# Feed-forward with standing weights: gated values come out transposed from the third block on

## The reference

```python
def swiglu(h, w1, w3, w2):
    return (jax.nn.silu(h @ w1) * (h @ w3)) @ w2
...
    h = rms_norm(x, norm_ffn[i]) * (1.0 + sc2) + sh2
    x = x + g2 * swiglu(h, ffn_w1[i], ffn_w3[i], ffn_w2[i])
```

## Time and profile before

| | |
|---|---|
| runs | 863.06 us median (862.61, 863.06, 865.84) |
| profiled execution | 863.67 us, its span 861.9 us |
| TensorE matmuls | 835.1 us busy, 97% of the span, 4254 instructions |
| weight loads | 697.2 us, 81% |
| VectorE | 611.7 us, 71% |
| ScalarE | 432.4 us, 50% |
| GpSimd | 123.7 us, 14% |
| DMA | 188.98 MB, mean 219 GB/s |
| chain that ended last | TensorE 81%, line 516 alone 66% |

### The profile page before, as it was taken

One profiled execution on the slowest core, in us unless ns is written; L12 is line 12 of the kernel. 1 busy time (PEld: TensorE's weight loads), 2 busy tenths in 40 slices (PEclk: granted clock), 3 DMA queues, 4 the chain that ended last, 5 costly groups with the idle time before them and its releaser, 6 DMA issues.

```text
span 861.9 us, 10974 instructions
## 1 busy us (share of the span) xinstructions
PE 835.1 (97%) x4254; PEld 697.2 (81%) x4254; DVE 611.7 (71%) x749; ACT 432.4 (50%) x549; POOL 123.7 (14%) x154
## 2 busy tenths in 40 slices
PE   4999999999999999999999999999999999999998
PEld 2778888878878987888888887888888788887886
DVE  4897798787888776577566685787867756644544
ACT  5365464454535666443344366778575635434431
POOL 3000101111110100011010000467810000000000
PEclk9899999999999999999999999999999999999999
DMA  9997888886977835688788755434254567765521
GB/s 320 366 357 249 284 275 269 281 256 219 281 260 241 263 115 189 190 277 294 253 278 267 248 169 173 147 103 143 98 179 129 182 220 244 243 201 170 191 97 50
DMA packets 122103, 188.98 MB, mean 219 GB/s; under 512 B 5683, under 2 KB 91048, under 8 KB 122052
## 3 DMA queue, kind: packets, MB, share of 16 engines
q1 hardware_dynamic: 109796, 146.10, 52.3%
q0 software_dynamic: 12256, 42.18, 14.6%
HBM read 187.18 MB, written 1.09 MB: 218 GB/s over the span
## 4 chain that ended last, share of the span: by engine, by line
PE 81%; DVE 9%; ACT 5%; issue 3%; DMA 1%; POOL 1%; SPq 0%; DVEq 0%; ACTq 0%; POOLq 0%
PE bank L516 66%; PE bank L632 2%; PE bank L738 2%; PE bank L712 2%; ACT whi L980 2%; DVE wlo L1355 2%; DVE acc L1376 1%; PE bank L907 1%; PE bank L585 1%; PE bank L851 1%; PE bank L693 1%; DMA x<-in_x_dram 1%; PE bank L582 1%; PE bank L721 1%; DVE wlo L1363 1%
## 5 line engine op out<-in xcount | busy, mean ns | idle before, releaser
L1355 DVE TENSOR_TENSOR wlo<-raw,whi 128x2048 fp32r<-128x2048 f32 x120 | 278.5, 2326 | 41.1 <-ACT whi L980 41.0
L980 ACT ACTIVATE whi<-raw 128x2048 fp32r<-128x2048 f32 (+1 forms) x124 | 235.6, 1901 | 22.8 <-DMA raw<-in_attn_w_qkv_dram 13.3
L516 PE MATMUL bank<-whi,hT_hi 128*128 128x512 f32 (+1 forms) x728 | 195.5, 392 | 0.9 <-DVE arena L1593 0.9
L516 PE MATMUL bank<-wlo,hT_hi 128*128 128x512 f32 (+1 forms) x752 | 195.0, 382 | 1.3 <-DVE wlo L1363 1.3
L516 PE MATMUL bank<-whi,hT_lo 128*128 128x512 f32 (+1 forms) x728 | 187.5, 380 | 0.0
L516 PEld LDWEIGHTS bank<-wlo,hT_hi 128*128 128x128 f32 x752 | 138.0, 189 | 30.3 <-DVE wlo L1363 2.5
L516 PEld LDWEIGHTS bank<-whi,hT_lo 128*128 128x128 f32 x728 | 133.2, 188 | 26.5
L516 PEld LDWEIGHTS bank<-whi,hT_hi 128*128 128x128 f32 x728 | 130.0, 189 | 27.4 <-issue 3.4
L393 POOL DMA_DIRECT2D ada_w<-in_ada_w_dram x80 | 42.6, 533 | 513.6 <-DVE acc L1376 496.4
L1376 DVE SCALAR_TENSOR_TENSOR acc<-ada_w,cact,acc 128x1024 f32<-128x1024 f32 x80 | 102.3, 1279 | 7.4 <-DMA ada_w<-in_ada_w_dram 5.1
L1216 ACT ACTIVATE arena<-bank 128x256 f32<-128x256 f32 x44 | 14.5, 381 | 166.9 <-PE bank L516 166.9
(11 more groups left out here) (185 smaller groups left out, 839.5 us busy)
## 6 DMA issues: line engine op xcount, KB each, us to landing
raw<-in_ffn_w_dram SPq DMA_DIRECT2D x88, 512.0 KB, 4.9
ada_w<-in_ada_w_dram POOLq DMA_DIRECT2D x80, 512.0 KB, 4.9
raw<-in_attn_w_qkv_dram SPq DMA_DIRECT2D x62, 512.0 KB, 6.4
raw<-in_ffn_w_dram SPq DMA_DIRECT2D x22, 1024.0 KB, 5.0
raw<-in_hgrn_w_in_dram SPq DMA_DIRECT2D x16, 1024.0 KB, 5.6
arena<-in_ada_w_dram SPq DMA_DIRECT2D x16, 512.0 KB, 10.3
raw<-in_attn_w_qkv_dram SPq DMA_DIRECT2D x4, 1024.0 KB, 7.6
raw<-in_attn_w_out_dram SPq DMA_DIRECT2D x4, 1024.0 KB, 6.7
```

What stands on the lines that cost most here:

```text
L516: mm = nc.tensor.matmul(dst[t][c][:, 0:n], lhs[:, k0 + k, t * P:(t + 1) * P], w[:, k, c * 512:c * 512 + n], start=start and k == 0, stop=s ...
L980: return nc.scalar.activation(dst, src, ACT.Copy)
L1355: nc.vector.tensor_tensor(wlo[:, m % RAW, :], raw[:, m % RAW, :], fp(hi_of(m)), ALU.subtract).then_inc(s["split"], 1)
```

## The change

For blocks 0 and 1 nothing changes (`NATURAL = 2`). For blocks 2 to 10 of each layer a gate unit is multiplied by the new function `hidden_unit`: the 128x128 blocks of the weights stand, and all 256 tokens of the activations move. The output has hidden columns on partitions: bank `gate_bank(j, 0)` holds hidden columns 0 to 127 of the block, `gate_bank(j, 1)` 128 to 255, each with the w1 product on the left and the w3 product on the right, for 256 tokens. A unit has 2 x 2 x 4 matmuls of 256 columns for each of its three products. `hidden_transposes` returns at once for these blocks; ScalarE and VectorE take the rounded part and the rest from `hid` in SBUF, and ScalarE waits for `f_hid` in place of `f_tr`. VectorE waits for its own `f_lo` before it writes `hid` again.

```diff
+NATURAL = 2
...
-        def hidden_bank(jt):
-
-            return bank[5] if jt == NF - 2 else bank[6]
+        def hidden_of(jt):
+
+            return hid[:, :, :] if jt >= NATURAL else bank[6][:].rearrange("p (k t) -> p k t", k=2)
...
                         if kind < 2:
-                            unit(base + r, hT_hi, hT_lo, 4, 4 * kind, 512, [[gate_bank(j, 0)], [gate_bank(j, 1)]],
-                                 kind == 0, kind == 1, tiles=(t,))
+                            if j < NATURAL:
+                                unit(base + r, hT_hi, hT_lo, 4, 4 * kind, 512, [[gate_bank(j, 0)], [gate_bank(j, 1)]],
+                                     kind == 0, kind == 1, tiles=(t,))
+                            elif t:
+                                hidden_unit(base + r, kind, j)
...
+            def hidden_unit(m, kind, j):
+
+                w = [v.rearrange("p (k n) -> p k n", k=4) for v in (hi_of(m), wlo[:, m % RAW, :])]
+
+                def product(w, h, start, stop):
+                    for b in range(2):
+                        for which in range(2):
+                            c = which * FC
+                            for k in range(4):
+                                mm = nc.tensor.matmul(gate_bank(j, b)[:, c:c + FC], w[:, k, c + b * P:c + (b + 1) * P],
+                                                      h[:, 4 * kind + k, :], start=start and which + k == 0,
+                                                      stop=stop and which + k == 4)
+                    return mm
+
+                pe.wait_ge(s["rounded"], m + 1)
+                product(w[0], hT_hi, kind == 0, False)
+                name, value = split_of(m)
+                pe.wait_ge(s[name], value)
+                product(w[1], hT_hi, False, False)
+                product(w[0], hT_lo, False, kind == 1).then_inc(s["pe_unit"], 1)
+
             def hidden_transposes(f, jt):
 
-                if jt is None:
+                if jt is None or jt >= NATURAL:
                     return
...
-                        act.wait_ge(s["f_tr"], n + 1)
+                        if jt < NATURAL:
+                            act.wait_ge(s["f_tr"], NATURAL * f + jt + 1)
+                        else:
+                            act.wait_ge(s["f_hid"], n + 1)
                         if n >= 4:
                             act.wait_ge(s["pe_unit"], base_of(n - 4) + 1)
-                        copy(hidT(oT_hi, n), hidden_bank(jt)[:].rearrange("p (k t) -> p k t", k=2)
-                             ).then_inc(s["f_hi"], 1)
+                        copy(hidT(oT_hi, n), hidden_of(jt)).then_inc(s["f_hi"], 1)
...
-                        nc.vector.tensor_tensor(hidT(oT_lo, n), hidden_bank(jt)[:].rearrange("p (k t) -> p k t", k=2),
-                                                fp(hidT(oT_hi, n)), ALU.subtract).then_inc(s["f_lo"], 1)
+                        nc.vector.tensor_tensor(hidT(oT_lo, n), hidden_of(jt), fp(hidT(oT_hi, n)), ALU.subtract
+                                                ).then_inc(s["f_lo"], 1)
...
                         if n:
-                            dve.wait_ge(s["f_tr"], n)
+                            dve.wait_ge(s["f_lo"], n)
```

More of the change, by code:

```diff
@@ L850, in hidden_transposes @@
                     for t in range(T):
-                        mm = nc.tensor.transpose(hidden_bank(jt)[:, k * SEQ + t * P:k * SEQ + (t + 1) * P],
+                        mm = nc.tensor.transpose(bank[6][:, k * SEQ + t * P:k * SEQ + (t + 1) * P],
                                                  hid[:, t, k * P:(k + 1) * P], ident[:])
```

## The result

The changed kernel takes 865.82 us (median of 15 runs, 863.63 to 869.27), the kernel before 862.25 us (15 runs). The ratio is 1.0034, 95% interval 1.0021 to 1.0047: slower by 2.9 us, between 1.8 and 4.1 (the two medians lie 3.6 us apart, inside that interval). The forecast was +2.9 us.

The account below looks back on a forecast made before the run. TensorE, busy 97% of the span, was taken to bound the kernel: +0.64 us for narrow matmuls less 0.48 for transposes, over 18 blocks +2.9 us, from 863.06 to 865.9 us (range 861.5 to 870.5).

Parts of the forecast that it names:

- The surplus: Gate units of blocks 2 to 10: each matmul costs 13 ns beyond its columns, so halving the width adds 0.64 us a block.
- The transposes: Feed-forward blocks 2 to 10: removing four transposes saves 0.48 us a block, more than their 0.44 us in the chain.
- The sum: Both feed-forwards: 0.64 - 0.48 = +0.16 us a block, +2.9 us over 18 blocks.
- The low bound: New gate units: at a weight-load floor of 0.109 us a matmul, -0.90 us a block, -16 us in all.
- The rest costs nothing: ScalarE's copy and VectorE's subtraction from SBUF: some 0.03 us more, hidden; 1.6 us left at a layer's last block.
- Rival A: Gate units: matmuls with standing weights run at the weight-load floor; 847 us, halfway 856; chance 6%.
- Rival B: Gate units: changing the output region costs 0.07 us at each product, 7.6 us on top, 873.5 us; chance 9%.
- Rival C: At the removed transposes: they were no cost, as TensorE waits there for something else; +11.5 us, 874.6 us; chance 3%.
- The rule of the Trainium skill: Gate matmuls: a warm one follows after N/2.4 + 2.5 ns, 109 ns for 256 columns; -6.4 us, 857 us.

Follow-up runs that it names:

- e2: The kernel before with only the transposes of blocks 2 to 10 left out (output not the reference's): 854.03 us, ratio 0.9903 to the kernel before.
- e5: Against the kernel before, blocks 2 to 8 keep weights standing while rounded activations and their rest move together, 512 columns past the high weights: 883.92 us, ratio 1.0256.
- e6: e5 with ScalarE taking the adaLN reductions out of bank 7 and TensorE waiting for that bank later: 860.97 us, ratio 0.9970 to the kernel before.
- e1: The changed kernel with the transposes of blocks 2 to 10 put back, into a bank nobody reads: 877.44 us, ratio 1.0177 to the kernel before.
- e7: e1 with block 9's unused transposes moved behind the first gate unit of block 10: 874.28 us, ratio 1.0129 to the kernel before.
- e3: The changed kernel with only the first 128 tokens moving in the new gate units, same weight loads: 860.61 us, ratio 0.9984 to the kernel before.
- e8: The changed kernel with only the first 192 tokens moving in the new gate units: 853.94 us, ratio 0.9889 to the kernel before.

## Why the prediction was right, point by point

- **The surplus doubles with the number of matmuls.** Forecast +0.64 us a block, from 0.120 us in rows of another unit with operands the other way round. Measured 11.51 against 10.88, +0.63; by e2 and the result together 11.3 us over 36 units, forecast 11.5. e5 and e6 have standing weights with 512 columns at the old pitch (16 in 3.63 us), so the operand that stands does not matter.
- **The transposes are worth 0.48 us, not the 0.44 of their piece.** e1's period has 0.48 more than the changed kernel's, and e2's 72 matmuls take 16.33 us where the period before was 16.80. e7 and e2 give 8.2 and 8.4 us for 18 (forecast 8.6); with their uncertainty these two alone could not tell 0.48 from 0.44.
- **The sum.** +2.9 us forecast, +2.9 (1.8 to 4.1) measured; 2.87 us of it in the two stretches of the trace. The term of an ordinary block was mis-sized by 0.02 us: the first wide matmuls behind narrow ones are a little late. 18 blocks at the measured +0.18 would be +3.2 us; the periods with adaLN reductions lengthen by less (in layer 0 from 18.62 to 18.68 and from 18.64 to 18.78 us, from w2 unit to w2 unit). So two small errors offset each other, and the match to a tenth is partly luck. So is that of the absolute 865.9 us: the kernel before came out at 862.25 us here, not at 863.06.
- **The low bound was too low.** I took 0.109 us from rows of 64 columns as the weight-load floor; here the floor is 0.112 (e3, e8). The forecast didn't rest on it, e3's expectation did.
- **The rest costs nothing.** ScalarE's copy from SBUF takes 0.63 us (forecast 0.632), VectorE's subtraction 0.68. At the end of layer 1 the timeline has the copy and the rest done at 846.9 and 849.3, against a consumer that needs them at 849.17 and 850.98: 1.7 us are left, where 1.6 were forecast.
- **One row was misread.** The prediction has the clock at nine tenths or more in every slice, but the second digit of `PEclk` in the earlier trace rows is 8. That slice ends at 43 us, far ahead of the feed-forwards, and nothing in the sum rests on it.
- **Rival A** (a pitch under 0.116) falls by the 1.92 us for 16. **Rival B** (slow returns to a bank) falls by the equal 1.91 to 1.92 us of all products. **Rival C** (another wait in the transposes' place) falls by e2.

These are the rows of the changed kernel for that last block:

```profile
849.17 1.07 PE L517 MATMUL bank<-whi,oT_hi 128*128 128x512 f32 x4
...
850.98 0.39 PE L517 MATMUL bank<-whi,oT_lo 128*128 128x512 f32 x1
...
846.25 0.63 ACT L1005 ACTIVATE oT_hi<-arena 128x512 fp32r<-128x512 f32 x1
...
848.61 0.68 DVE L1711 TENSOR_TENSOR oT_lo<-arena,oT_hi 128x512 fp32r<-128x512 f32 x1
```

The rule of the Trainium skill that I weighed ("TensorE: Matmul & The Clock Gate", Back-to-back issue gap), which that section gives for isolated matmuls and not for a stream with weight loads, made an estimated 857 us (18 x -0.36 is -6.5 us and not -6.4; the 857 stands). The changed kernel, at 0.120 us for 256 columns where the rule has 0.109, doesn't bear it out. The Trainium skill's rule for weight loads ("TensorE: Matmul & The Clock Gate", LDWEIGHTS: columns over 1.2 GHz) makes an estimated 107 ns for 128 columns, 5 ns under the 112 of e3 and e8.

## What to carry to other kernels

Where TensorE has no idle time, count matmuls as well as columns. Here each one of 256 or 512 columns cost its columns plus 13 ns, and swapping operands so that the moving width halves cost more (11.3 us) than the removed transposes gave back (8.2 to 8.4 us). Before removing a small step, price it with what it does to its neighbours (0.48 us against a piece of 0.44). When a new form takes another PSUM bank, look for who else uses that bank and which queue empties it: that wait cost up to 5.9 us a time, and a less loaded engine and a later wait together took all of it away.

## What the runs showed of the hardware that was not expected

TensorE's granted clock fell to the lower of its two levels while it was busy without a gap. In e3 (128 columns moving) it stood at 0.50 from about 453 to 473 us. The fall came 16 narrow matmuls behind the 16 matmuls of one column (449.34 in the rows of e3), and the clock rose again within the next w2 unit; in e8 (192 columns) it fell in the same place for one product; in the changed kernel, with 256 columns, the same place kept the full clock:

```profile
455.00:470.00 15.00, 15.00 (x121) 1.00 0.73 238
```

Other stretches of 96 matmuls of 128 columns kept the full clock too (10.67 us each). What tells them apart was not tried and stays open.
